# Sample attention in quarters of a pair's keys, with two pairs in flight

## The reference

```python
def _sample_attention(q, qi, wi, k_new, v_new, kidx_new, pool_k, pool_v, pool_kidx, page_table):
    ...
    sc = _index_scores(qi, wi, kidx_all)                 # 2048 past + 8 new positions
    sc = jnp.where(key_pos <= qpos, sc, NEG_INF)
    _, idx = lax.top_k(sc, 256)
    ...                                                  # rows of pool_k, pool_v by page_table, or of k_new, v_new
    logits = jnp.einsum('btkgd,btnkd->btkgn', qg, k_sel) * HEAD_DIM ** -0.5
    p = jax.nn.softmax(logits, axis=-1)
    o = jnp.einsum('btkgn,btnkd->btkgd', p, v_sel)
```

## Time and profile before

| | us |
|---|---|
| three runs | 3567.05, 3570.57, 3573.18 (median 3570.57) |
| the profiled execution: time | 3570.03 |
| its span | 3568.2 |
| PE busy | 3431.7 (96%) |
| VectorE (DVE) busy | 2079.8 (58%) |
| ScalarE (ACT) busy | 1190.8 (33%) |
| GpSimd (POOL) busy | 841.4 (24%) |

### The profile page before, as it was taken

The page is one execution under the profiler, slowest core; times in us unless marked ns, Lnnn a source line. Parts: engine busy times, 40 slices in busy tenths (PEclk is TensorE's granted clock), DMA queues, the critical chain, the costliest instruction groups (busy, mean ns, idle before and its releaser), DMA issues.

```text
span 3568.2 us, 44307 instructions
## 1 busy us (share of the span) xinstructions
PE 3431.7 (96%) x16753; PEld 2765.8 (78%) x16753; DVE 2079.8 (58%) x3959; ACT 1190.8 (33%) x2161; POOL 841.4 (24%) x785
## 2 busy tenths in 40 slices
PE   7899999999889999999999999999999999999999
PEld 6779888854577778887877688888877678887887
DVE  2463499300064489911533899935534899997652
ACT  2345442333253242213621622124422632115531
POOL 2235564410055003301230033111220023111011
PEclk9999999989899999999999999999999999999999
DMA  8555566744237635564066255660076245660007
GB/s 225 181 197 189 179 227 241 259 167 177 96 133 238 217 127 190 192 227 168 16 233 213 99 182 195 210 219 15 12 244 210 84 154 189 209 230 33 10 13 239
DMA packets 274100, 592.28 MB, mean 166 GB/s; under 512 B 16957, under 2 KB 198391, under 8 KB 222178
## 3 DMA queue, kind: packets, MB, share of 16 engines
q1 hardware_dynamic: 270434, 551.70, 45.5%
q0 software_dynamic: 3456, 37.75, 2.9%
HBM read 448.93 MB, written 140.47 MB: 165 GB/s over the span
## 4 chain that ended last, share of the span: by engine, by line
PE 76%; DVE 13%; issue 4%; ACT 2%; DMA 2%; POOL 1%; SPq 1%; ACTq 0%; DVEq 0%; POOLq 0%
PE ps L1015 71%; DVE JUNK L1668 7%; PE ps L1020 5%; DVE SC L1610 1%; POOL BBL L2028 1%; DVE SMALL L1672 0%; DMA GB<-gb_scratch 0%; ACT T L703 0%; DVE GE L1670 0%; DMA q_scratch<-QO 0%; SPq L426 0%; DMA WR<-in_w_proj_a 0%; DVE sL L1714 0%; ACT JUNK L622 0%; DVE PFX L1694 0%
## 5 line engine op out<-in xcount | busy, mean ns | idle before, releaser
L1015 PE MATMUL ps<-HTH,WLH 128*128 128x512 f32 x4672 | 1479.8, 393 | 0.0
L1015 PEld LDWEIGHTS ps<-HTH,WLH 128*128 128x128 f32 x4672 | 879.7, 188 | 187.1 <-issue 6.5
L1015 PE MATMUL ps<-HTL,WLH 128*128 128x512 f32 x2336 | 911.9, 390 | 0.0
L1668 DVE TENSOR_SCALAR_CACHE_REDUCE JUNK<-SC,SMALL 128x384 bf16<-128x384 f32 (+13 forms) x392 | 580.0, 1480 | 15.7 <-POOL sSC L1949 1.8
L1015 PEld LDWEIGHTS ps<-HTL,WLH 128*128 128x128 f32 x2336 | 440.1, 188 | 93.7 <-issue 6.5
L1741 DVE CUSTOM_DVE_ANT_0 LP<-ps,SC 128x512 f32<-128x512 f32 (+3 forms) x320 | 187.5, 609 | 345.4 <-PE ps L1015 282.2
L773 ACT ACTIVATE T<-ps 128x512 f32<-128x512 f32 x192 | 114.8, 598 | 692.6 <-PE ps L1015 692.6
L1891 POOL TENSOR_TENSOR WLH<-WR,WLH 128x1024 fp32r<-128x1024 f32 x97 | 233.3, 2405 | 407.6 <-ACT WLH L612 407.3
L1015 PE MATMUL ps<-T,V 128*128 128x256 f32 x1088 | 284.5, 389 | 6.3 <-ACT T L891 6.3
L1015 PEld LDWEIGHTS ps<-T,V 128*128 128x128 f32 x1088 | 188.3, 192 | 34.8 <-ACT T L891 12.9
L612 ACT ACTIVATE WLH<-WR 128x1024 fp32r<-128x1024 f32 x97 | 102.7, 1059 | 279.5 <-DMA WR<-in_w_in 200.2
(11 more groups left out here) (314 smaller groups left out, 5043.8 us busy)
## 6 DMA issues: line engine op xcount, KB each, us to landing
WLH<-w_scratch SPq DMA_DIRECT2D x291, 1024.0 KB, 4.9
w_scratch<-WLH SPq DMA_DIRECT2D x97, 1024.0 KB, 6.3
WR<-in_w_in SPq DMA_DIRECT2D x73, 512.0 KB, 4.3
MW<-in_w_mod SPq DMA_DIRECT2D x24, 512.0 KB, 7.1
XN<-in_x_prompt SPq DMA_DIRECT2D x4, 2048.0 KB, 9.3
q_scratch<-QO SPq DMA_DIRECT2D x32, 256.0 KB, 5.6
ma_scratch<-T SPq DMA_DIRECT2D x32, 256.0 KB, 5.6
gb_scratch<-GB SPq DMA_DIRECT2D x32, 256.0 KB, 6.0
```

The lines of the kernel that those rows point to most:

```text
L1015: return pe.matmul(out, lhsT, rhs, start=start, stop=stop, **more)
L1668: link(dve.tensor_scalar(JUNK[0:n, 0:row.shape[1]], row, MID[0:n, c:c + 1], 0.0, ALU.is_ge, ALU.add, accum_out=CNT[0:n, c:c + 1]))
```

## The change

The stage becomes steps of a quarter (`c`) of a pair's keys, and the steps of pair `u` are interleaved with those of pair `u - 1`: in a step PE makes the logits of `(u, c)`, turns the keys of the next quarter, turns the probabilities of `(u - 1, c)` and multiplies them with their values. A loop of five stages runs over the four pairs; the first has no values, the last nothing else.

- The mask is added by PE: it opens each logits bank with the product of `sSEL` and the scaled mask `sBIAS`, both fp32r now, and the logits accumulate on top. `sBX`, its copies and VectorE's addition go; VectorE only looks for the largest (`largest`), and ScalarE takes the exponential straight from PSUM in five pieces (`probabilities`), whose sums VectorE adds.
- The copies of turned keys are shared between ScalarE (groups 0 and 2) and VectorE (1 and 3), into 8 tiles `sKPT` of a quarter's key head each.
- Pages are gathered in quarters, 4 KB per partition and 512 KB each, by a table `QROW` with four indices per row, into 16 slots; 64 gathers in place of 16. The first four are issued during the projections (item 20 of `PROJ_B`), the others where all stood.

The core of the diff:

```diff
-    sBX = at("sBX", [P, PAST + NS], F32, rS + 8192 + 4352 + 8448)
+    sBIAS = at("sBIAS", [NS, PAST + NS], F32R, rS + 8192 + 4352)
+    sL = at("sL", [P, PAST + NS], F32, rS + 8192 + 4352 + 8448)
-    sPG = [at(f"sPG{i}", [P, RUN, KV * HD], F32, a) for i, a in enumerate((rH, rH + 16384, rW))]
-    sKPT = at("sKPT", [P, PAST], F32, rW + 16384)
-    sL = at("sL", [P, PAST + NS], F32, rM)
+    sPG = [at(f"sPG{i}", [P, RUN // 4, KV * HD], F32, a) for i, a in enumerate(
+        [rM + 4096 * i for i in range(4)] + [rH + 4096 * i for i in range(8)] + [rW + 4096 * i for i in range(4)])]
+    sKPT = [at(f"sKPT{i}", [P, TILE], F32, a) for i, a in enumerate(
+        [rW + 16384 + 2048 * i for i in range(4)] + [rB + 16384 + a for a in (2048, 4096, 10240, 12288)])]
...
-    PAGE_USES = [(what, 2 * u + e) for u in PAIRS for what in "kv" for e in range(2)]
-    page_slot = lambda *use: PAGE_USES.index(use) % 3
-    KEY_GROUPS = [(e, kv, c) for e in range(2) for kv in range(KV) for c in range(4)]
+    GROUPS = [(e, kv) for e in range(2) for kv in range(KV)]
+    PAGE_USES = [("k", 0, 0, 0), ("k", 0, 0, 1)]
+    for u in range(NSEQ // 2 + 1):
+        for c in range(4):
+            after = (u, c + 1) if c < 3 else (u + 1, 0)
+            PAGE_USES += [("k", *after, e) for e in range(2) if after[0] in PAIRS]
+            PAGE_USES += [("v", u - 1, c, e) for e in range(2) if u]
+    page_slot = lambda *use: PAGE_USES.index(use) % 16
+    key_slot = lambda c, g: 4 * (c % 2) + g
...
 # ScalarE
-                act.activation(sSC[:, :], sSC[:, :], ACT.Copy, scale=-NEG).then_inc(*biased.mark(t, "S"))
+                act.activation(sBIAS[:, :], sSC[:, :], ACT.Copy, scale=-NEG).then_inc(*biased.mark(t, "S"))
...
+            def probabilities(u, c):
+                n = TILE if c < 4 else NS
+                if c == 4:
+                    act.wait_ge(*s_row_max.at(u))
+                act.activation(sL[:, c * TILE:c * TILE + n], ps[c][:, 0:n], ACT.Exp, bias=NM[:, 0, 0:1],
+                               accum_out=ABS[:, c:c + 1]).then_inc(*s_exp.mark(u, c))
...
+            keys(0, 0)
+            for u in range(len(PAIRS) + 1):
+                for c in range(4):
+                    if c < 3 and u in PAIRS:
+                        keys(u, c + 1)
+                    elif u + 1 in PAIRS:
+                        keys(u + 1, 0)
+                    if u:
+                        if c == 0:
+                            turned(u - 1, 4)
+                        turned(u - 1, c)
+                if u in PAIRS:
+                    for c in (4, 0, 1, 2, 3):
+                        probabilities(u, c)
...
 # TensorE
+            def turn_bank(*key):
+                b = 5 + turns[0] % 2
+                turns[0] += 1
...
+            def keys(u, c):
+                for g, (e, kv) in enumerate(GROUPS):
+                    slot = page_slot("k", u, c, e)
+                    pe.wait_ge(*pg_in[slot].at("k", u, c, e))
+                    b = turn_bank("s_kt", u, c, g)
+                    for i in range(4):
+                        ins_ = turn(ps[b][:, i * P:(i + 1) * P], sPG[slot][:, i, kv * HD:(kv + 1) * HD])
...
+            def logits(u, c):
+                claim(c)
...
+                mm(ps[c][:, 0:n], sSEL[u // 2][:, u % 2, :], rows, True, False, skip_group_check=True)
+                for g, (e, kv) in enumerate(GROUPS):
...
+                    ins_ = mm(ps[c][r:r + 32, 0:n], query(u, e, kv), sKPT[key_slot(c, g)][:, :] if c < 4 else sKT[:, kv, :],
+                              False, True, skip_group_check=True)
+                ins_.then_inc(*s_qk.mark(u, c))
+                freed[c] = s_exp.at(u, c)
...
+            keys(0, 0)
+            for u in range(len(PAIRS) + 1):
+                for c in range(4):
+                    if u in PAIRS:
+                        logits(u, c)
+                        if c == 3:
+                            logits(u, 4)
+                    if c < 3 and u in PAIRS:
+                        keys(u, c + 1)
+                    elif u + 1 in PAIRS:
+                        keys(u + 1, 0)
+                    if u:
+                        if c == 0:
+                            if u >= 2:
+                                turn_back(u - 2)
+                            turn_probabilities(u - 1, 4)
+                        turn_probabilities(u - 1, c)
+                        if c == 0:
+                            values(u - 1, 4)
+                        values(u - 1, c)
+            turn_back(PAIRS[-1])
...
 # VectorE
+        for c in range(4):
+            ins_ = dve.tensor_scalar(QROWF[:, c, :], TABLEF[:, :], 4.0, float(c), ALU.mult, ALU.add)
+        link(ins_)
+        dve.tensor_copy(QROW[:, :, :], QROWF[:, :, :])
...
+                    dve.tensor_copy(sKPT[key_slot(c, g)][:, :], ps[bank("s_kt", u, c, g)][:, :]).then_inc(*s_kt_dve.mark(u, c, g))
+            def largest(u, c):
+                n = TILE if c < 4 else NS
+                dve.wait_ge(*s_qk.at(u, c))
+                ins_ = dve.tensor_reduce(LO[:, c:c + 1], ps[c][:, 0:n], AX_X, ALU.max)
+                if c == 4:
+                    link(ins_)
+                    dve.tensor_reduce(NM[:, 0, 0:1], LO[:, 0:5], AX_X, ALU.max, negate=True).then_inc(*s_row_max.mark(u))
...
 # GpSimd
-            what, s = PAGE_USES[n]
-            if n < 3:
+            what, u, c, e = PAGE_USES[n]
+            if n < 4:
+                pool.wait_ge(*kx_t.at(NSEQ - 1, 3))
+            elif n < 16:
                 pool.wait_ge(*product.at(AFTER_PAGES[0] - 1, "S"))
...
+                before, u0, c0, e0 = PAGE_USES[n - 16]
+                pool.wait_ge(*(s_kt.at(u0, c0, 2 * e0 + 1) if before == "k" else s_pv.at(u0, c0)))
+            rows = ins["cache_" + what][0].rearrange("n (c r) h d -> (n c) (r h d)", c=4 * PER_PAGE)
...
+                if t == 0 and i == SAMPLE_ITEMS + 4:
+                    for n in range(4):
+                        gather_pages(n)
```

More of the change, by code:

```diff
@@ L310, in program @@
     kx_in = [signal(f"kx_in{i}", 16) for i in range(2)]
-    pg_in = [signal(f"pg_in{i}", 16) for i in range(3)]
+    pg_in = [signal(f"pg_in{i}", 16) for i in range(16)]
     q_out = [signal(f"q_out{i}", 16) for i in range(2)]
@@ new lines, in turned @@
+            def turned(u, c):
+                act.wait_ge(*s_pt.at(u, c))
+                src = ps[bank("s_pt", u, c)]
+                if c < 4:
+                    ins_ = act.activation(sPT[:, 4 * c:4 * c + 4, :], src[:, :].rearrange("p (a b) -> p a b", a=4), ACT.Copy)
+                else:
+                    if u == 0:
+                        act.wait_ge(*ma_out[0].at(0, KC - 2))
+                        act.wait_ge(*ma_out[1].at(0, KC - 1))
+                    ins_ = act.activation(sPTN[:, :], src[0:NS, 0:P], ACT.Copy)
+                ins_.then_inc(*s_pt_copy.mark(u, c))
@@ L1728, in sample_attention @@
                 ins_.then_inc(*s_attn.mark(u))
+            keys(0, 0)
+            for u in range(len(PAIRS) + 1):
+                for c in range(4):
+                    if u in PAIRS:
+                        largest(u, c)
+                        if c == 3:
+                            largest(u, 4)
+                    if c < 3 and u in PAIRS:
+                        keys(u, c + 1)
+                    elif u + 1 in PAIRS:
+                        keys(u + 1, 0)
+                    if u and c == 0:
+                        if u >= 2:
+                            put(u - 2)
+                        dve.wait_ge(*s_exp.at(u - 1, 3))
+                        link(dve.tensor_reduce(SUM[:, 0, 0:1], ABS[:, 0:5], AX_X, ALU.add))
+                        link(dve.reciprocal(RIN[:, 0, 0:1], SUM[:, 0, 0:1]))
+                if u:
+                    scale(u - 1)
+            put(PAIRS[-1])
         def mask_logits(t, u):
@@ L1908, in gather_pages @@
         def gather_pages(n):
[L1909 to L1910 removed]
+            what, u, c, e = PAGE_USES[n]
+            if n < 4:
+                pool.wait_ge(*kx_t.at(NSEQ - 1, 3))
+            elif n < 16:
                 pool.wait_ge(*product.at(AFTER_PAGES[0] - 1, "S"))
[L1913 to L1919 removed]
+                if n >= 12:
+                    for j in range(AFTER_PAGES[0] - 3, AFTER_PAGES[0]):
+                        pool.wait_ge(*w_out[j % 3].at(j))
+            else:
+                before, u0, c0, e0 = PAGE_USES[n - 16]
+                pool.wait_ge(*(s_kt.at(u0, c0, 2 * e0 + 1) if before == "k" else s_pv.at(u0, c0)))
+            rows = ins["cache_" + what][0].rearrange("n (c r) h d -> (n c) (r h d)", c=4 * PER_PAGE)
+            s = 2 * u + e
+            pool.indirect_dma_start(sPG[n % 16][:, :, :].rearrange("p i d -> p (i d)"), None, rows,
+                                    bass.IndirectOffsetOnAxis(ap=QROW[:, c, s:s + 1], axis=0)).then_inc(*pg_in[n % 16].mark(*PAGE_USES[n]))
         def h_low(t):
@@ L2073, in _ @@
             if t == 0:
-                for n in range(len(PAGE_USES)):
+                for n in range(4, len(PAGE_USES)):
```

179 lines of the change are left out of this document (71 added, 108 removed).

## The result

| | before | after |
|---|---|---|
| median (us) | 3570.64 | 3465.53 |
| all runs | 3567.05 to 3573.18 | 3464.39 to 3469.35 |
| span of the profiled execution | 3568.2 | 3462.5 |

The ratio is 0.9711, with a 95% interval of 0.9699 to 0.9722.

What follows compares the result with a forecast made beforehand. PE bounds the sample attention by what it executes plus where it waits. Its new steps end the value products 34.5 us earlier, less 0.7 for index instructions: 3570.03 - 33.8 = 3536.2, forecast 3537 us, range 3527 to 3560.

Steps and rivals of the forecast that it cites:

- Logits, 0.98 + 3 x 0.87: In each step of the sample attention, four logits products in a row on PE take 3.59 us.
- Values, "The order among them changes, the records do not": A quarter's value products on PE, 32 of a pair's 136 records, take 3.33 us of the old 14.16.
- Mask, 0.24: The fp32r mask product ahead of each step's logits takes 0.24 us, with bounds of 0 and 0.43.
- Turns, 4.0: Four key turns and one of probabilities, sharing two PSUM banks, take 4.0 us per step for 2.9 of work.
- Start of the stage, first logits' end at 748.8: Key turns begin after the mask's scaling at 740.54; the first logits start at the lower clock and end at 748.8.
- First exponentials: 2.6 us of waiting and a clock that falls: Before overwriting the first logits bank, PE idles about 2.6 us; 1.5 us more for a falling clock.
- Early gathers, 0, upper end 5: Four gathers moved into the projections delay a weight split PE never waits for: 0 us, at most 5.
- The other gathers, no wait: The other 60 gathers take 75 us of an otherwise idle queue; PE waits nowhere on a gather.
- dearer hand-overs: Rival: bank hand-overs between turns cost 0.27 us more each, 13 us over 16 steps, perhaps another 5; 3555 us, chance 0.22.
- The clock did not fall in the steps: Rival: turning and waiting bring the 1.2 GHz level in every step, 8.3 us more each; 3669 us, chance 0.07.
- No gather was late: Rival: page gathers too slow, 60 one at a time taking 354 us, values 131 late; 3701 us, chance 0.04.
- better than the sum: Case: banks back at once and no clock fall at the first exponentials, some 8 us more; 3529 us, below 3527 chance 0.05.

Runs made afterwards that it cites:

- the run without the stride: The changed kernel with the scaled mask written in key-block order, so that the mask product reads 512 neighbouring values per row; 3465.2 us.
- the run with the early table: The changed kernel with ScalarE's exponential table loaded behind the first quarter's copies and a pair's exponentials in the order 0, 4, 1, 2, 3; 3464.1 us.

## Why the prediction was wrong

The reading of the profile held: PE bounds the stage, and what its steps cost is what the stage costs. The steps themselves, in the prediction's order:

- **Logits, 0.98 + 3 x 0.87.** Failed: 0.99 for all four. The 0.87 of the earlier trace rows is the price of two products of one group, which write to the same strip; the new step has four products of four groups. 2.60 x 16 = 41.6 us. (That is by the price of a steady step; in the first stage, right behind the last key copies, the four took 1.22, and at the lower clock up to 1.97.)
- **Values, "The order among them changes, the records do not".** Failed, and this is the sentence at which the forecast went wrong: it took the mean of 136 records, 0.104, as the price of any record, when it was the price of records that share a strip. 1.01 for 3.33: 2.32 x 16 = 37.1 us. The diff showed the four groups taking turns in the inner loop.
- **Mask, 0.24.** Too low: 0.61, outside both ends (0 and 0.43); 5.9 us the other way.
- **Turns, 4.0.** Right: 4.16, with the forecast wait of 0.7 for the probabilities' copy measured at 0.69; in the 11 steps that turn both, 11 x 0.16 = 1.8.
- **Start of the stage, first logits' end at 748.8.** 748.54, though by luck, as two errors met: 1.97 for the four logits products instead of 5.22, and a start 2.8 us later. All four ran at the lower clock, where the prediction let it rise halfway; the earlier trace rows does not show such a rise within 5 us (0.60 and 0.53 over 11.9 us).
- **First exponentials: 2.6 us of waiting and a clock that falls.** Right: 2.54, then 0.68 until 777. The fall cost 2.1 where 1.5 was put: the step took 9.50 from its mask product to the next, its like in the next stage 7.39.
- **Early gathers, 0, upper end 5.** It was the upper side: 3.1 us, seen where the prediction said a wait would show.
- **The other gathers, no wait.** Right.

41.6 + 37.1 - 5.9 - 1.8 - 3.1 = 67.9 of the 71.8 us between the forecast 33.8 and the 105.6 that lie between the two profiled executions. The new tokens' logits give 1.7 more (0.48 in place of 0.9, four times). Some 2 us are not assigned; what follows the last division took 2.4 less than before, which is within what executions differ by there.

The rivals: of dearer hand-overs there is no sign in the turns. The clock did not fall in the steps (1.00 from 777 to 846), so the rule of the Trainium skill (TensorE: Matmul & The Clock Gate, "A second HAM failure mode: psum-queue depth-cycling"), which the prediction weighed at 3669, is not borne out here. No gather was late. None of the three lay on the side where the time came out; the case "better than the sum" did, with 8 us from other causes.

The Trainium skill has the rule that was missed (TensorEngine Tiling (Array Packing), "Theoretical Speedup" and "Tiling Modes"): with at most 32 stationary columns the array can work as four tiles side by side, each tied to its own PSUM partitions, up to four times as fast. The runs agree: 0.99 for four logits products and 0.97 for one; 1.01 for 32 value records on four strips and 3.61 on one.

## What to carry to other kernels

Before a price per instruction is carried from an old order to a new one, look at what stood beside it: here products with 32 stationary columns that write to one strip of partitions ran one after another, and on different strips they shared their time. Where a kernel has such products in several independent groups, let the groups take turns in the innermost loop; for the values, in the kernel before, this alone, a change of a few lines, was worth 35 of the 105 us. And a transfer that is moved into "idle" time can delay what runs there: look for the next load that the critical engine needs.

## What was not expected of the hardware

- The same wait did not always cost the clock. After 2.54 us ahead of the second pair's logits it read 0.74 between 764 and 777 in the changed kernel, 1.00 in the run without the stride; after 0.82 us in the run with the early table 0.87.
- A read of one value in sixteen made ScalarE's pass over 2048 columns 3.64 us, where 2112 neighbouring ones took 1.95. PE's pass over 512 columns was 0.61 with that stride and 0.43 without.
